# Modulation dot products moved to the first feed-forward, and four input sums moved from VectorE to GpSimd, in a two-layer diffusion backbone

## The reference

```python
s0, sc0, g0, s1, sc1, g1, s2, sc2, g2 = split(silu(c) @ w_ada[l] + b_ada[l], 9)
n = rmsnorm(h, norm_g[l, 0]) * (1 + sc0) + s0
h = h + 0.5 * g0 * swiglu(n, w_ffn_up[l, 0], w_ffn_down[l, 0])    # D_MODEL 1024, D_FF 2816
n = rmsnorm(h, norm_g[l, 1]) * (1 + sc1) + s1
h = h + g1 * token_mix(n)
n = rmsnorm(h, norm_g[l, 2]) * (1 + sc2) + s2
h = h + 0.5 * g2 * swiglu(n, w_ffn_up[l, 1], w_ffn_down[l, 1])
```

## Time and profile before

| | |
|---|---|
| median of three runs | 3138.71 us (3136.15 to 3142.4) |
| the profiled execution | 3137.54 us, its span 3135.4 us |
| PE busy | 3018.9 us, 96% of the span |
| DVE busy | 2122.9 us, 68% |
| ACT busy | 1141.8 us, 36% |
| POOL busy | 85.8 us, 3% (164 instructions, nearly all DMA issues) |

### The profile page before, as it was taken

One profiled execution on the slowest core, in us unless ns is written; L12 is line 12 of the kernel. 1 busy time (PEld: TensorE's weight loads), 2 busy tenths in 40 slices (PEclk: granted clock), 3 DMA queues, 4 the chain that ended last, 5 costly groups with the idle time before them and its releaser, 6 DMA issues.

```text
span 3135.4 us, 48664 instructions
## 1 busy us (share of the span) xinstructions
PE 3018.9 (96%) x19892; PEld 2938.2 (94%) x19892; DVE 2122.9 (68%) x3521; ACT 1141.8 (36%) x1820; POOL 85.8 (3%) x164
## 2 busy tenths in 40 slices
PE   7999999998999999999999999999899999999998
PEld 4899999997899999999999999999789999999998
DVE  7666666646655557988968988863565556785675
ACT  3422312422444433434343433442154443443432
POOL 0000000000000000000000000000000000000000
PEclk8999999999999999999999999999999999999999
DMA  8255553345122532444322434334521242122222
GB/s 304 91 202 228 213 190 135 115 153 221 67 75 85 192 112 80 135 141 142 122 95 94 149 121 142 108 114 163 224 82 71 76 186 108 68 95 81 95 68 75
DMA packets 89743, 408.90 MB, mean 130 GB/s; under 512 B 10049, under 2 KB 13569, under 8 KB 68914
## 3 DMA queue, kind: packets, MB, share of 16 engines
q1 hardware_dynamic: 60384, 285.76, 25.6%
q0 software_dynamic: 19872, 94.53, 8.3%
q10 hardware_dynamic: 9266, 25.50, 2.2%
HBM read 359.46 MB, written 46.30 MB: 129 GB/s over the span
## 4 chain that ended last, share of the span: by engine, by line
PE 77%; DVE 14%; ACT 4%; issue 3%; DMA 1%; ACTq 0%; DVEq 0%
PE tile_psum L743 21%; PE misc_psum L860 12%; PE tile_psum L750 11%; PE misc_psum L864 6%; PE tile_psum L1215 6%; PE tile_psum L704 3%; PE tile_psum L1219 3%; PE misc_psum L669 3%; PE tile_psum L669 2%; PE tile_psum L860 2%; PE tile_psum L709 2%; PE tile_psum L1080 1%; DVE h L2254 1%; DVE wlo L2083 1%; PE tile_psum L864 1%
## 5 line engine op out<-in xcount | busy, mean ns | idle before, releaser
L743 PE MATMUL tile_psum<-n_hi,whi 128*128 128x320 f32 x1536 | 352.3, 311 | 4.0 <-issue 2.2
L743 PE MATMUL tile_psum<-n_lo,whi 128*128 128x320 f32 x1536 | 350.1, 309 | 0.0
L2083 DVE TENSOR_TENSOR wlo<-raw,whi 128x2048 fp32r<-128x2048 f32 (+4 forms) x130 | 250.6, 1930 | 114.2 <-ACT whi L1491 112.2
L743 PE MATMUL tile_psum<-x_hi,whi 128*128 128x320 f32 x1300 | 300.1, 312 | 17.4 <-DVE h L2254 11.7
L743 PE MATMUL tile_psum<-x_lo,whi 128*128 128x320 f32 x1300 | 298.3, 311 | 0.0
L743 PEld LDWEIGHTS tile_psum<-n_hi,whi 128*128 128x128 f32 x1536 | 257.6, 189 | 6.8 <-DVE n_lo L2174 4.2
L743 PEld LDWEIGHTS tile_psum<-n_lo,whi 128*128 128x128 f32 x1536 | 258.2, 189 | 0.0
L1491 ACT ACTIVATE whi<-raw 128x2048 fp32r<-128x2048 f32 (+4 forms) x130 | 208.9, 1616 | 126.7 <-DMA raw<-in_w_down 43.7
L1215 PE MATMUL tile_psum<-n_hi,whi 128*128 128x320 f32 x768 | 237.4, 320 | 11.0 <-ACT gate_out L1978 10.3
L2254 DVE SCALAR_TENSOR_TENSOR h<-tile_psum,ada_t,h 128x320 f32<-128x320 f32 (+2 forms) x408 | 154.2, 434 | 129.2 <-PE tile_psum L750 127.5
L750 PE MATMUL tile_psum<-n_hi,wlo 128*128 128x320 f32 x1536 | 241.3, 309 | 0.0
(11 more groups left out here) (384 smaller groups left out, 6450.1 us busy)
## 6 DMA issues: line engine op xcount, KB each, us to landing
w_ada<-in_w_ada POOLq DMA_DIRECT2D x72, 512.0 KB, 4.0
raw<-in_w_up SPq DMA_DIRECT2D x72, 512.0 KB, 3.8
raw<-in_w_up SPq DMA_DIRECT2D x34, 1024.0 KB, 4.9
w_ada<-in_w_ada SPq DMA_DIRECT2D x56, 512.0 KB, 6.3
raw<-in_w_gate SPq DMA_DIRECT2D x24, 1024.0 KB, 4.9
raw<-in_w_down SPq DMA_DIRECT2D x29, 768.0 KB, 4.4
whi<-table_keep SPq DMA_DIRECT2D x20, 1024.0 KB, 4.7
wlo<-table_keep SPq DMA_DIRECT2D x20, 1024.0 KB, 6.9
```

Source lines behind the costliest of these rows:

```text
L743: pe.matmul(tps[:, t.s, m, 0:TH], blk(p, m * n + k)[0], (hi, lo)[b][:, k, tok], start=k == 0 and b == 0, stop=False)
L2083: ins = dve.tensor_tensor(lo_at(r, n)[:, 0:w], raw_at(r, n)[:, 0:w], hi_at(h_, n)[:, 0:w].bitcast(F32), ALU.subtract)
```

## The change

It has two parts. First, `ADA_PLAN` is another table. In (0, 0) the steps do 70 tiles in place of 56: chunk 1's eight up panels and four of chunk 2's do three tiles each where they did two, and the last two up panels of chunk 0 do two where they did one. (0, 1) and (1, 0) do 29 each in place of 36 and none in their chunk 0. SP issues only the first two of these loads; all others are issued by GpSimd, in (0, 0) between the stores of the tables. Second, `n_sum` runs on GpSimd (`input_sums`), with a wait for the last `n_lo`, and before sum 3 one for the last `x_lo` of chunk 0. DVE now makes the low parts of sums 0 and 2 behind half (3, 1), and before low part 1 waits for all four sums.

```diff
-ADA_PLAN = {(0, 0): [0, 0, 2, 2, 2, 2, 1, 1] + [2] * 4 + [2] * 8 + [2] * 4 + [2] * 6 + [1, 1, 0, 0],
-            (0, 1): [0, 0, 1, 1] + [1] * 4 + [1] * 6 + [2, 2, 1, 1] + [1] * 6 + [2, 2, 1, 1] + [1] * 6 + [0] * 4,
+ADA_PLAN = {(0, 0): [0, 0, 2, 2, 2, 2, 2, 2] + [2] * 4 + [3] * 8 + [2] * 4 + [3, 3, 3, 3, 2, 2] + [1, 1, 0, 0],
+            (0, 1): [0] * 8 + [1] * 6 + [2, 2, 1, 0] + [1] * 6 + [2, 2, 1, 0] + [2] + [1] * 5 + [0] * 4,
...
+            def input_sums(l, f):
...
+                pool.wait_ge(n_ready, NORM_READY[l, f])
+                n_sum(0, [(h21, add, h22), (add, l21), (add, l22)])
+                n_sum(2, [(h21, sub, h11), (add, l21), (sub, l11)])
+                n_sum(1, [(sub, h11), (sub, l11)], sum_raw[0])
+                pool.wait_ge(hid_ready, HIDDEN_FIRST[l, f])
+                n_sum(3, [(h12, sub, sum_raw[1]), (add, l12)])
...
+            def ada_loads(n):
...
+                    pool.wait_ge(ada_used, t - 1)
+                    pool.dma_start(adaw[:, t % 2, :], w_ada[t]).then_inc(ada_late[t % 2], 16)
+
             for p, kind in enumerate(KINDS):
-                if kind == "prepare":
...
+                if p < FIRST_MIX:
+                    ada_loads(ADA_STEP[p] if late[0] + ADA_STEP[p] <= ADA_LATE else ADA_LATE - late[0])
+                if KINDS[p + 1:p + 2] == ["prepare"]:
...
                     if l == 0:
...
+                        for f_ in ((0, 1), (1, 0)):
+                            input_sums(*f_)
+                            ada_loads(sum(ADA_PLAN[f_]))
+                    else:
+                        input_sums(1, 1)
...
             def n_sum_low(i):
+                if i < 2:
+                    dve.wait_ge(n_sums, 4 * (fast[0] // 18) + 3 + i)
                 lo_part(sum_lo[i], sum_raw[i], sum_hi[i], n_sum_lo, n_sum_hi)
...
-                            if (i, j) == (0, 1):
-                                n_sum(0, [(h21, add, h22), (add, l21), (add, l22)])
-                            if (i, j) == (1, 1):
-                                n_sum(2, [(h21, sub, h11), (add, l21), (sub, l11)])
-                            if (i, j) == (2, 1):
-                                n_sum(1, [(sub, h11), (sub, l11)], sum_raw[0])
+                            if (i, j) == (3, 1):
                                 n_sum_low(0)
-                            if (i, j) == (3, 0):
                                 n_sum_low(2)
...
                         if c == 0 and i == 0:
-                            n_sum(3, [(h12, sub, sum_raw[1]), (add, l12)])
                             n_sum_low(1)
```

More of the change, by code:

```diff
@@ L235 @@
 ADA_LATE = ADA_EARLY + sum(ADA_PLAN[0, 0])
+FIRST_MIX = KINDS.index("mix")
+NORM_READY = {(0, 1): 7 * KT, (1, 0): 9 * KT, (1, 1): 14 * KT}
+HIDDEN_FIRST = {lf: 2 * sum(CHUNKS) + e * (2 * FAST_CHUNKS[0] + sum(FAST_CHUNKS[1:]) + 3) + 2 * FAST_CHUNKS[0]
+                for e, lf in enumerate(((0, 1), (1, 0), (1, 1)))}
 ADA_BY = [min(ADA_EARLY + n, DEPTH * ADA_TILES) for n in accumulate([0] + ADA_STEP)]
@@ L1322, in ada_load @@
                     t = tiles_in[0]
-                    if t == ADA_LATE:
+                    if t == ADA_EARLY + 2:
                         return
@@ L1431, in _, with own, n_block @@
             pool.dma_start(sm_keep[1], sml[:, :].bitcast(F32)).then_inc(small_kept, 16)
-            for p, kind in enumerate(KINDS):
-                if kind == "prepare":
-                    s, t = p % SLOTS, PREPARE_OF[p]
-                    pool.wait_ge(hi_ready, ROUNDED[p])
+            def own(ins):
+                ins.then_inc(sum_step, 1)
+                pool.wait_ge(sum_step, due(sum_step))
+            def n_block(m, k, x_):
+                return x_[:, 4 * k:4 * k + 4, m * TH:(m + 1) * TH].bitcast(F32)
@@ new lines, in n_sum @@
+            def n_sum(i, parts, start=None):
+                out = sum_raw[i]
+                if start is None:
+                    (a, op, b), parts = parts[0], parts[1:]
+                    own(pool.tensor_tensor(out, a, b, op))
+                    start = out
+                for op, b in parts[:-1]:
+                    own(pool.tensor_tensor(out, start, b, op))
+                    start = out
+                op, b = parts[-1]
+                pool.tensor_tensor(out, start, b, op).then_inc(n_sums, 1)
+                pool.wait_ge(n_sums, due(n_sums))
@@ new lines, in input_sums @@
+            def input_sums(l, f):
+                add, sub = ALU.add, ALU.subtract
+                h11, h12, h21, h22 = [n_block(m, k, nh) for m in range(2) for k in range(2)]
+                l11, l12, l21, l22 = [n_block(m, k, nl) for m in range(2) for k in range(2)]
+                pool.wait_ge(n_ready, NORM_READY[l, f])
[4 more added lines that the diff above has]
+                n_sum(3, [(h12, sub, sum_raw[1]), (add, l12)])
@@ new lines, in _ @@
+            late = [ADA_EARLY + 2]
+            def ada_loads(n):
+                for _ in range(n):
+                    t = late[0]
+                    if t == DEPTH * ADA_TILES:
+                        return
+                    late[0] += 1
+                    if t == ADA_LATE:
+                        pool.wait_ge(y_done, KT)
+                    pool.wait_ge(ada_used, t - 1)
+                    pool.dma_start(adaw[:, t % 2, :], w_ada[t]).then_inc(ada_late[t % 2], 16)
+            for p, kind in enumerate(KINDS):
+                if p < FIRST_MIX:
+                    ada_loads(ADA_STEP[p] if late[0] + ADA_STEP[p] <= ADA_LATE else ADA_LATE - late[0])
+                if KINDS[p + 1:p + 2] == ["prepare"]:
+                    s, t = (p + 1) % SLOTS, PREPARE_OF[p + 1]
+                    pool.wait_ge(hi_ready, ROUNDED[p + 1])
@@ L2423, in fast_up @@
                 junk_at[0] = junk_down
[L2425 to L2440, removed]
             def n_sum_low(i):
+                if i < 2:
+                    dve.wait_ge(n_sums, 4 * (fast[0] // 18) + 3 + i)
                 lo_part(sum_lo[i], sum_raw[i], sum_hi[i], n_sum_lo, n_sum_hi)
             def fast_ffn(l, f, norm, m1, last):
-                add, sub = ALU.add, ALU.subtract
-                h11, h12, h21, h22 = [n_block(m, k, nh) for m in range(2) for k in range(2)]
-                l11, l12, l21, l22 = [n_block(m, k, nl) for m in range(2) for k in range(2)]
                 plan, section = ADA_PLAN[l, f], 2 if f == 0 else 8
```

7 lines of the change are left out of this document (4 added, 3 removed).

## The result

The changed kernel takes 3175.61 us (median of four runs, 3171.0 to 3178.55) against 3137.64 for the kernel before on the same chip: a ratio of 1.0117, interval 1.0099 to 1.0135. It is slower by 38 us. The profiled span is 3176.7 us, 41.3 more than before.

A forecast was written before the change was run, and what follows sets the result against it. PE was taken as the bound in (0, 0), crowded DVE in short chunk 0 stretches of (0, 1) and (1, 0). A loss of 39.5 less a gain of 18 gave +21.5 us: 3160 us, range 3142 to 3184.

The forecast's parts named there:

- L: Time from start to landing of the third tile's load in (0, 0): 5.3 us taken, ends 4.0 and 6.5.
- Rival 1: In (0, 0) the third tile is hidden and only the gain of 18 us stays: 3121 us; chance 10%.
- The round of 11.2 + L: DVE's chain per three-tile panel in (0, 0): 16.5 us against PE's 14.08, 2.4 us over.
- The 39.5 us of (0, 0): Loss from third tiles in twelve panels of (0, 0): 29.8 us in chunk 1, 9.7 in chunk 2.
- PE's slower clock behind such waits adds nothing here: In (0, 0), slower PE matmuls behind waits add nothing, since PE then waits for DVE anyway.
- about 40: Sign looked for: PE's waits from 270 to 500 us in the changed profile total about 40 us.
- The tables' term: In chunk 1 of (0, 0), three table splits, hidden before, add 3.5 us each, 10.5 us.
- The tables' stores: In (0, 0) the stores stand one panel (14 us) later, adding nothing in the sum.
- The gain in the fast feed-forwards: Chunk 0 of (0, 1), (1, 0) and (1, 1), sums and tiles off DVE: near 18 us, between 5 and 21.
- g: Time of one GpSimd sum instruction in chunk 0: 3.0 us taken, ends 1.49 and 4.5.
- the wait of 1.0 us in each: PE's remaining wait because of sum 3 in chunk 0 of (0, 1), (1, 0) and (1, 1): 1.0 us each.
- rival 2: GpSimd's sums get in DVE's way in chunk 0: 5.5 us in each of three stretches, 3174 us; chance 15%.

The follow-up runs named there:

- e2: The changed kernel with the third tile done behind the next half's multiply, same number of tiles: 3150.45 us, ratio 1.0043.
- e5: The changed kernel with the old tile table and the sums on VectorE, leaving only GpSimd's tile loads and the stores' places: 3138.81 us, ratio 1.0003.
- e6: The changed kernel with GpSimd storing each table ahead of that panel's tile loads: 3184.15 us, ratio 1.0149.
- e3: The changed kernel with the sums back on VectorE at their old places and the third tile behind the next half's multiply: 3143.01 us, ratio 1.0021.
- e7: e3 with the tables' stores ahead of the tile loads, as in e6: 3132.33 us, ratio 0.9988.
- e8: The changed kernel with only sum 3 made by VectorE again, at its old place: 3168.44 us (one run).
- e4: The changed kernel with GpSimd's ten additions and subtractions replaced by memsets of the same size: 3160.48 us (one run).

## Why the prediction was right, and where its sizes were off

**Direction and mechanism: right.** DVE idles ahead of all twelve third tiles, with the tile's DMA as releaser, PE waits for DVE's multiply, and without that order (e2) chunk 2's loss is zero. The forecast's L of 5.3 us is 5.5 in the mean. The waits are 1.5 to 6.7 us, where 2 to 4 were looked for. Rival 1 is ruled out: DVE was 64% busy in chunk 1 (72.56 of 113) and still the bound. The round of 11.2 + L, and 3.5 more with a table, fits the rows: with a wait for the tile of about 2 us (L of 4.3) the rounds are 15.5 and 15.9 us without a table and 19.0 and 19.1 with one, and with a wait of 4.57 (L of 6.9) 18.0.

**The 39.5 us of (0, 0): the term that was mis-sized is L, one value for twelve loads.** It came to 47.3 (33.8 + 13.5). Chunk 1's first panel costs 6.3 us in place of 2.5, since its L is 9.0 (6.72 + 2.29): 3.8 more. Its seven other rounds cost 25.0 (123.5 us from 304.82 to 428.34, less 7 x 14.08) where 16.8 + 10.5 were forecast: 2.3 less. Chunk 2 costs 14.0 up to its last wait where 9.7 were forecast, since its four waits are 3.9 us in the mean, an L of 6.2: 4.3 more, of which 0.5 is won back behind it. Why the first load, and chunk 2's, took longer than the others isn't known. The last 2.5 us are the next point.

**"PE's slower clock behind such waits adds nothing here": nearly right.** PE's matmuls took some 13 us more than before in the halves behind its waits. Nearly all of that lies in time in which DVE was late anyway, so that it shortened PE's next wait and not the round: PE's waits are 32.7 us, below the "about 40" that the prediction looked for, while the loss is above it. It counts where no wait follows. Behind the last wait of chunk 1 PE starts at 428.88, 2.5 us are lost to the clock (0.50 from 428 to 434 us), and none are given back; behind chunk 2's last it is 0.1; and once in between DVE waited 0.95 us for PE's half. That is 3.6 us of 47.3.

**The tables' term (3.5 us in each of three panels): right.** With nearly the same wait for the tile (1.47 to 2.03 us) the two rounds with a table take 19.04 and 19.13 us, the two without one 15.85 and 15.47. PE's waits don't show it as plainly (4.78 and 4.64 us, but 1.97 behind the first table, since the slow half ahead of it had already used 2.8 us of that round's 5.0).

**The tables' stores: "nothing in the sum": right for this change, wrong as a rule.** They cost nothing with two tiles a step (e5). In the change no wait of DVE for a rounded panel is over 2.0 us; early stores even made it slower (e6). Once the third tile stood apart they cost 8.4 us (e3's column a, 22.6, against e7's 14.2). What e7's 14.2 are made of was not taken apart further: PE's waits are 8.6 us of them, and DVE still waits for nine tiles there, 14.9 us in all.

**The gain in the fast feed-forwards: 18 forecast, 11.3 measured** (7.1 + 6.8 - 2.6). g was right for the first three instructions: 2.94 to 3.08 us, 3.0 taken. The Trainium skill ("GPSIMD Engine Reference", 3.1) has a factor of 1.96 between the two engines, an estimate of 2.9 from DVE's 1.49, and these rows agree. But sum 3's two took 4.07 and 4.05, beside DVE's low parts. The `ISA` row cost nothing: GpSimd stood idle 105 us ahead of the first sum. The term that failed is the wait of 1.0 us in each: it was 3.4, in two pieces of 1.75 and 1.66, though at full clock, and only (1, 1) shows the loss openly, as +2.6. The step that was wrong is that DVE has nothing else to do ahead of the update and merely waits for sum 3: from the end of the last `x_lo` (1291.35) to the update at 1302.10 it has no gap, with its own low parts stretched from 2.88 to 5.64 and the next `wlo` from 1.22 to 2.91. The mechanism is rival 2's, two engines that hold each other up, and beside it the low parts that the change had moved behind the last half (e8). Rival 2's price of 5.5 was too high, since the clock did not fall; its sum 3, 9.0 us behind the last `x_lo`, was near the measured 8.3. Its time of 3174 is next to the measured one, but by other terms: it had 13.5 us more than the forecast here, where 6.7 was so, and the longer loads in (0, 0) and the mixers made the rest. So its figure is right by luck. The forecast, 3160, was 16 us low and the range held the time; 5.4 of the 41.3 us lie in the mixers, which it had at nothing.

The Trainium skill ("SBUF — State Buffer", Who interferes with whom) says that a DVE instruction with two SBUF inputs contends with a GpSimd one that reads SBUF, and not with one that only writes it. The change's rows and e4's agree: `hidden`, whose second input is in PSUM, keeps its 0.49 us throughout, and `x_lo` does not. By that rule rival 2 deserved more than 15%.

The measured sum: 47.3 in (0, 0), -11.3 in the fast ones, +5.4 in the mixers, -0.1 elsewhere, 41.3 us.

## What to carry to other kernels

When work is put into an engine's idle time, ask what stands behind it in that engine's queue: a load that starts only when its own step begins puts its whole landing time ahead of the next multiply, and three changed lines (e2) took 24 us of 38 back. A sum moved to GpSimd isn't free where VectorE's instructions beside it read two operands from SBUF and have no slack: the earlier sums stretched such rows at no cost, sum 3 did not. Time that PE loses to a slower clock while it would have waited anyway must not be added to the waits: compare VectorE's rounds, not PE's waits plus PE's slowness. And when a wait is removed, expect the one that it hid: here the tile's wait hid the slot that a late store kept, and only both orders together, with the sums on VectorE (e7), came out below the kernel before, by 0.12%.

## What the runs showed of the hardware

- A subtraction of 128 x 320 on DVE took 0.49 us with GpSimd idle and 0.75 to 2.37 beside its additions; one of 128 x 1024 took 1.21 and up to 4.02. Of GpSimd's ten instructions of 128 x 1280 in (0, 1), six took 2.94 to 3.13 and four 3.85 to 4.89.
- A GpSimd memset of 128 x 1280 took 1.17 us and stretched none of DVE's rows beside it.
- A tile load of 512 KB behind two stores of 1 MB in one queue was used 9.0 us after its issue (e6), where that kernel's median landing from 270 to 560 us is 5.3.
- PE's waits of 1.75 and 1.66 us left the granted clock at 1.00; that of 6.15 us was followed by some 5.5 us of matmuls at half speed (0.73 us for two in place of 0.46), the 1.2 GHz level; behind that of 4.64 us the granted clock from 428 to 434 us is 0.50.
